# Summing the head norms of a gated linear attention with two reduced-precision products, one head later

## The reference, cut to what matters

```
o_f = gla_chunked(qh, kh, vh, af)
o_b = flip(gla_chunked(flip(qh), flip(kh), flip(vh), flip(ab)))
o = o_f + o_b
o = o * lax.rsqrt(jnp.mean(o * o, axis=-1, keepdims=True) + EPS) * gla_head_norm.astype(jnp.float32)
...
y_b = jax.nn.silu(go) * o
y = jnp.concatenate([y_a, y_b], axis=-1)
return y @ w_out
```

## Time and profile before

| | |
|---|---|
| median of 3 runs | 1728.21 us (1727.53 to 1728.27) |
| the profiled execution | 1729.34 us |
| its span in the profile | 1727.5 us |
| TensorE busy | 1705.1 us (99%) |
| VectorE busy | 1251.5 us (72%) |
| ScalarE busy | 808.3 us (47%) |
| GpSimd busy | 355.5 us (21%) |

### The profile page before, as it was taken

One profiled execution on the slowest core, in us unless ns is written; L12 is line 12 of the kernel. 1 busy time (PEld: TensorE's weight loads), 2 busy tenths in 40 slices (PEclk: granted clock), 3 DMA queues, 4 the chain that ended last, 5 costly groups with the idle time before them and its releaser, 6 DMA issues.

```text
span 1727.5 us, 21399 instructions
## 1 busy us (share of the span) xinstructions
PE 1705.1 (99%) x8156; PEld 1402.5 (81%) x8156; DVE 1251.5 (72%) x1603; ACT 808.3 (47%) x1090; POOL 355.5 (21%) x155
## 2 busy tenths in 40 slices
PE   7999999999999999999999999999999999999998
PEld 5888888878888788888888888877888888888787
DVE  6564677858899889999887679946476767676534
ACT  5332322245335555555554456423366566666522
POOL 3366565264100000000000000221321211211051
PEclk9999999999999999999999999999999999999999
DMA  5333222135411236555576334412311111102232
GB/s 186 110 110 110 86 86 85 35 119 171 139 64 60 86 107 209 202 177 192 176 257 217 110 109 168 163 55 73 110 43 37 37 38 36 49 22 76 80 134 98
DMA packets 72957, 190.99 MB, mean 111 GB/s; under 512 B 8992, under 2 KB 11424, under 8 KB 72864
## 3 DMA queue, kind: packets, MB, share of 16 engines
q1 hardware_dynamic: 53568, 138.76, 24.5%
q10 hardware_dynamic: 19296, 50.97, 7.9%
HBM read 139.89 MB, written 49.81 MB: 110 GB/s over the span
## 4 chain that ended last, share of the span: by engine, by line
PE 90%; DVE 5%; ACT 2%; issue 1%; DMA 1%; ACTq 0%; DVEq 0%
PE psum L871 21%; PE psum L1175 17%; PE psum L1206 9%; PE psum L910 7%; PE psum L1316 7%; PE psum L1343 5%; PE psum L1063 5%; PE psum L1243 4%; PE psum L1352 4%; PE psum L1332 3%; PE psum L892 1%; PE psum L1268 1%; PE psum L1452 1%; PE psum L924 1%; PE psum L1009 1%
## 5 line engine op out<-in xcount | busy, mean ns | idle before, releaser
L782 POOL TENSOR_TENSOR wl<-wstage,wh 128x1024 fp32r<-128x1024 f32 x64 | 165.4, 2585 | 792.3 <-ACT wh L1479 763.1
L777 POOL TENSOR_TENSOR wh<-wstage,ones 128x1024 fp32r<-128x1024 f32 x43 | 103.1, 2398 | 458.1 <-PE psum L1316 295.6
L871 PE MATMUL psum<-hh,wh 128*128 128x512 f32 x544 | 172.7, 399 | 0.0
L871 PE MATMUL psum<-hl,wh 128*128 128x512 f32 x544 | 167.8, 390 | 0.0
L871 PE MATMUL psum<-hh,wl 128*128 128x512 f32 x544 | 167.6, 389 | 0.0
L2403 DVE SCALAR_TENSOR_TENSOR cc<-uu,col,cc 128x1023 f32<-128x1023 f32 x88 | 113.0, 1284 | 16.8 <-ACT cc L1699 15.2
L2738 DVE TENSOR_TENSOR ptl<-psum,pth 128x512 fp32r<-128x512 f32 x128 | 82.5, 686 | 57.0 <-ACT pth L2006 56.9
L871 PEld LDWEIGHTS psum<-hh,wh 128*128 128x128 f32 x544 | 100.2, 188 | 24.8 <-issue 2.9
L871 PEld LDWEIGHTS psum<-hl,wh 128*128 128x128 f32 x544 | 102.1, 188 | 21.6
L871 PEld LDWEIGHTS psum<-hh,wl 128*128 128x128 f32 x544 | 102.1, 188 | 21.6
L2006 ACT ACTIVATE pth<-psum 128x1024 fp32r<-128x1024 f32 x64 | 65.3, 1021 | 80.4 <-PE psum L1332 80.4
(11 more groups left out here) (428 smaller groups left out, 4440.6 us busy)
## 6 DMA issues: line engine op xcount, KB each, us to landing
wstage<-w_units SPq DMA_DIRECT2D x116, 512.0 KB, 3.6
acts<-cc ACTq DMA_DIRECT2D x22, 512.0 KB, 2.6
yo<-w_units SPq DMA_DIRECT2D x22, 512.0 KB, 7.2
down_sums<-yo SPq DMA_DIRECT2D x22, 512.0 KB, 8.7
wstage<-down_sums SPq DMA_DIRECT2D x44, 256.0 KB, 2.7
wstage<-w_units SPq DMA_DIRECT2D x35, 256.0 KB, 2.9
mix<-spill ACTq DMA_DIRECT2D x12, 512.0 KB, 2.6
kq<-mix SPq DMA_DIRECT2D x16, 256.0 KB, 3.9
```

The source lines that it names most:

```text
L777: pool.tensor_tensor(high, stage(u), ones[:, :].unsqueeze(1).to_broadcast([P, 8, P]), ALU.mult).then_inc(w_high, 1)
L782: pool.tensor_tensor(low, stage(u), high.bitcast(F32), ALU.subtract).then_inc(w_split, 1)
L871: mm = pe.matmul(out[:, t], w[:, wslot, b, :], x[part][:, xk, t], start=start and n == 0, stop=stop and n == 2)
```

## The change

The square of a head's output is split into a high part (fp32r, made by ACT into the unused tile `yah[:, 3, :]`) and a low part (fp32r, made by DVE over the square itself, in `sql`, which lies on `sq`), and the sum over partitions is made of two fp32r products with the ones, four matmuls in all. The sum of head h now stands within the units of head h + 1, ahead of their step 1; that of the last head stands within the output projection, behind the first three k of its first tile. The other pieces move: `scores1` from step 2 to 4, `keys` from 4 to 5, `values` from 6 to 8, `sums` from 10 to 11; `scores0` and `output` stay.

```diff
-GLA_AT = {0: "scores0", 2: "scores1", 4: "keys", 6: "values", 10: "sums", 21: "output", 23: "norm"}
+GLA_AT = {0: "scores0", 1: "norm", 4: "scores1", 5: "keys", 8: "values", 11: "sums", 21: "output"}
...
-        sq = sb("sq", [P, 2, T])
+        sq, = over(("sq", [P, 2, T], F32))
+        sql, = over(("sql", [P, 2, T], F32R))
+        sb("region0", [P, 2 * T])
...
+        osq_high, osq_low = sums_made, w_sum
...
             def gla_norm(h):
 
-                pe.wait_ge(osq_ready, h + 1)
-                sums(slot(3), sq[:, 0, :]).then_inc(osum_done, 1)
+                pe.wait_ge(osq_low, OSQ + h + 1)
+                for n, x in enumerate((yah[:, 3, :], sql[:, 0, :])):
+                    for half in range(2):
+                        t = slice(half * HT, half * HT + HT)
+                        mm = pe.matmul(slot(3)[:, t], ones[:, :].bitcast(F32R), x[:, t], start=n == 0, stop=n == 1)
+                mm.then_inc(osum_done, 1)
...
-                else:
-                    gla_norm(h)
+                elif h:
+                    gla_norm(h - 1)
...
             for ks in ((0, 1, 2), (4,), (3,), (5,), (6,)):
                 for m in range(3):
                     out_half(0, m, ks)
+                    if m == ks[0] == 0:
+                        gla_norm(HEADS - 1)
...
                 act.activation(sq[:, 0, :], slot(2), ACT.Square).then_inc(osq_ready, 1)
+                act.wait_ge(osq_ready, h + 1)
+                act.activation(yah[:, 3, :], sq[:, 0, :], ACT.Copy).then_inc(osq_high, 1)
...
+            def square_low(h):
+                dve.wait_ge(osq_high, OSQ + h + 1)
+                dve.tensor_tensor(sql[:, 0, :], sq[:, 0, :], f32(yah[:, 3, :]), ALU.subtract).then_inc(osq_low, 1)
+
             for h in range(HEADS):
+                if h:
+                    square_low(h - 1)
                 masked(h, 0)
                 masked(h, 1)
...
                 convolved(h)
+            square_low(HEADS - 1)
             gated_conv(HEADS - 1)
```

More of the change, by code:

```diff
@@ L66 @@
 SW_RIGHT = {"P1": "B11", "P2": "B21", "P3": "B22", "P4": "T4", "P5": "T1", "P6": "T2", "P7": "T3"}
-RANKS = 2
+OSQ = 2
+RANKS = OSQ + HEADS
 LEFT_AT = ((0, 0), (1, 0), (1, 1), (0, 1))
```

## The result

| | before | after |
|---|---|---|
| median of the runs | 1728.24 us (4 runs) | 1737.40 us (1734.17 to 1737.88, 4 runs) |
| the profiled execution | 1729.34 us | 1737.88 us |
| its span | 1727.5 us | 1736.0 us |

The change makes the kernel slower, by half a percent: the ratio is 1.0048, 95% interval 1.0037 to 1.006. The forecast was 1734.4, within 1728.5 to 1737.5: the right side, inside the range by 0.1 us, and 3.0 us too low.

The account below looks back on a forecast made before the run. PE was taken to bound the kernel, busy 1705.1 of 1727.5 us. The loop 3.7 us later (7.4 lost, 3.7 saved) plus 2.5 behind it gave 6.2 us, so 1734.4 us, range 1728.5 to 1737.5.

Parts of the forecast that it names:

- Work taken out: Sums on PE: 1.06 us saved for each of heads 0 to 2, 0.8 for the last, waits of 0.5; 4.5 saved.
- Head 1: At output of head 1: DVE's states end at 236.1, PE comes at 234.4 and waits 1.7 us.
- Border to head 2: scores0 waits 0.2 for qi, the sum 1.8 for DVE's low part of the square; 2.0 us lost.
- border to head 1: Sum of head 0: high part done at 198.1, low part at 199.4, PE comes at about 200.7; no wait.
- Output of head 2: In head 2, output waits for DVE's states as in head 1; 1.7 us lost.
- Behind the last head: Behind the loop: the moved sum and its root delay ACT's third-tile weights and PE's k = 3; 2.5 us later.
- Border to head 3: The same waits as at the border to head 2 come again; 2.0 us lost.
- I take the clock as it is: Whole kernel: PE stays busy, so nothing lets its clock fall; no time counted for it.
- mild: Rival: DVE's low part gets the port ahead of POOL at both borders; 2.6 us slower, 1730.8; chance 0.24.
- one more product of POOL at a border: At each of two borders, one more POOL product ahead of DVE's low part adds 2.4 us.

Follow-up runs that it names:

- e5: The changed kernel with the three edits of e2, e3 and e4 together; median 1724.04 us, ratio 0.9974 to the kernel before.
- e10: The changed kernel with POOL waiting for DVE's low part of the convolution before it splits the next weights; median 1732.23 us, ratio 1.0021 to the kernel before.
- e4: The changed kernel with POOL waiting at head borders for DVE's low part of the square before splitting weights; median 1731.45 us, ratio 1.0016 to the kernel before.
- e2: The changed kernel with ACT's last root put behind the high part of the third output tile's weights; median 1735.02 us, ratio 1.0033 to the kernel before.
- e1: The changed kernel run again with no edit; median 1737.52 us, ratio 1.0045 to the kernel before.
- e11: The changed kernel run a third time with no edit, for the clock; median 1737.92 us.
- e6: The changed kernel's table, places and order with the sum in 32 bits, no high or low part; median 1739.73 us, ratio 1.0068 to the kernel before.
- e12: The kernel of e6 run a second time with no edit, for the clock; four runs of 1734.99, 1735.74, 1737.99 and 1739.02 us.
- e3: The changed kernel with scores1 at step 3, keys at 4, values at 6, sums at 10; median 1730.02 us, ratio 1.001 to the kernel before.
- e9: Kernel before with the square rounded once, one one-pass product, sums of heads 0 to 2 moved behind the border; median 1721.92 us, ratio 0.9961.

## Why the prediction was right, and where not

- *Work taken out, 4.5 us.* Right: sums of 0.91 to 0.94 us; and e5, where only a wait of 0.5 is left, gains 4.2.
- *Head 1.* Right: the forecast was states done at 236.1 and a wait of 1.7; they are done at 235.9 and PE waits 1.76. The low part of the convolution is held as worked out (done at 217.1, forecast 217.3), and e10 shows its share by itself.
- *Border to head 2.* Right: DVE's low part was to be done at 250.5 behind the tap addition and POOL's weights, in that order; it is done at 250.2, and PE waits 1.65 (1.8 forecast). At the border to head 1, no wait, as forecast. e4 shows that POOL's weights hold it.
- *Output of head 2, 1.7.* Right: 1.76.
- *Behind the last head, 2.5 us.* Right: 1.4 and 1.1 of wait (1.6 and 1.3 forecast), and e2 takes 2.5 off.
- *Border to head 3, 2.0.* Wrong, and this is the step that failed: "I take the clock as it is (PE stays busy, so nothing lets it fall)". The prediction put waits of 1.7 to 1.8 us on PE and did not ask what they do to the clock, so the term stood at nothing. The clock fell for 10 us behind the third of them. From the start of `output` to the start of the second pair of the step behind it PE takes 295.28 - 285.76 = 9.5 us where the same takes 5.9 in head 1, so 3.6 more, and 1.2 more until 298; of these 4.8 the border gives 1.8 back, since ACT, DVE and POOL went on at their speed and the sum no longer waits. That leaves 3.0. The runs agree: the two executions whose clock stayed up took 1734.17 and 1734.20, beside the forecast of 1734.4, and the others some 3.2 more.

The prediction quoted the Trainium skill, "SBUF — State Buffer", section "SBUF: two separate sides": a VectorE operation with two SBUF inputs and a GpSimd operation that reads SBUF exclude each other. The rows here agree: with POOL out of the way the low parts take 1.21 and 1.23, beside it 3.40 and 2.40, POOL's remaining time and their own. Among the rivals, "mild" asked for the low part going first; e4 brings that about, and the time is 1731.45, against the 1730.8 worked out for it.

The waits came out well because each engine's order was followed with the durations of the trace, and each operation with two SBUF inputs on DVE was set against POOL's at the same microsecond. That the measured median lies inside the range is luck in part: the upper end of 1737.5 was there for one more product of POOL at a border, which did not come, and it covers a fall of the clock by 0.1 us; e1 and e11, the same kernel, have medians just above it (1737.52 and 1737.92).

What stays open: why the clock falls behind the same waits in one execution and not in the next, and why in the changed kernel it fell in the output of head 2 in every profiled execution, in e6 in that of head 1. e4 has the two waits of 1.8 without the third and, by the mean clocks, no such fall in ten executions; e6 and e12 have the same two and it fell in six of eight. What does keep it away is known only by result: with the waits for the states gone (e3) or at 0.6 (e10) no execution of 10 and 11 has a mean clock as low as with the fall. No experiment here tells what decides.

## What to carry to other kernels

When a step is moved, follow what hangs on the steps behind it in the table, not the step itself: the sum was free to move (e9), and the two steps by which the scores moved with it cost more than the sum saved (e3, e6). Set every two-input SBUF operation of VectorE against GpSimd's operations at the same time; one wait of GpSimd for the operation that PE needs first took 6 us off here, more than half of it because the clock stayed up. And ask whether the added operation must be there: rounding the square once, with neither copy nor low part, gained as much as the split done right, where a norm made from rounded squares is good enough.

## What had not been expected of the hardware

A wait of TensorE of about 1.8 us, on an engine that is 98% busy over the launch, can be followed by 10 us at the lower clock (1.2 in place of 2.4 GHz), and then costs PE 4.7 us beyond the wait itself (e6 against e12). In whole launches it showed as 3.1 to 3.2 us (within e12, and in the changed kernel, where a later wait shrinks for it). The Trainium skill, "TensorE: Matmul & The Clock Gate", section "Part 1: The HAM clock gate", says that the array's clock is gated by how busy TensorE has been recently, and that at the start of a kernel the number of slow matmuls differs from run to run. These runs show such a difference between executions of one program in the middle of a kernel, behind a wait.

Two engines that shut each other out took turns when both had work waiting: at 243 to 250 us of the changed kernel the order was POOL's `qi`, DVE's tap addition, POOL's weights, DVE's low part, so that an operation of 1.2 us ended 3.4 us after DVE was free for it.
